# Indexed attention heads: where the softmax reciprocal is applied, in a one-core two-layer trunk

## The chip, the cores and the metric

The kernel runs on one core of a Trainium2 chip. The metric is the device time of one execution in microseconds (us). TensorE (PE) multiplies, VectorE (DVE), ScalarE (ACT) and GpSimd (POOL) do the rest, SyncE (SP) issues most DMAs. Engines run their own instruction streams in order and meet through semaphores. PE writes to eight PSUM banks of 128 partitions by 512 float32.

## The reference

Two decoder layers over 512 tokens of width 1024. Layer 0 mixes 8 forgetting-attention heads (A) with 8 sliding-window heads (B); layer 1 mixes 8 indexed sparse heads (C) with 8 latent heads (D). Each layer then has a squared-ReLU MLP. The part that the change touches is the sparse attention:

```python
logits = jnp.einsum("bqhd,bqkd->bqhk", qb, k_sel) * (d ** -0.5)
logits = jnp.where((dist >= 0)[:, :, None, :], logits + bias, -jnp.inf)
p = jax.nn.softmax(logits, axis=-1)
out = jnp.einsum("bqhk,bqkd->bqhd", p.astype(v_c.dtype), v_sel)
```

Softmax divides each query's exponentials by their sum. The kernel doesn't gather: it scores all causal keys and adds a mask that leaves the selected ones.

## The kernel before, in words

Heads are numbered j = 0 to 31 in the order A, B, D, C, so the indexed heads are j = 24 to 31. Queries lie in four blocks of 128, and a block q attends to its q+1 key blocks, so a head has ten 128x128 blocks of probabilities with queries on the partitions. For `probabilities times values` they must lie with keys on the partitions, so each of the ten is turned on PE into PSUM (`turn_probs`, L993). Precise float32 products are made of rounded halves: a value is split by ACT into a high part and by DVE or POOL into the low rest.

One head passes these stages:

- PE `scores(j)` (L928) into banks 0 to 2; it waits until the exponentials of head j-1 have left each bank.
- DVE `maxima(j)` (L2349): four instructions add the bias strip and find the row maxima, one per query block.
- ACT `exponentials(j)` (L1545) write `probs` and the row sums `expsum`.
- DVE `sums(j)` (L2372) makes the reciprocals `rsum`.
- POOL `diagonal(j)` (L1885), for D and C heads, writes `diag[j % 2]`: four 128x128 diagonal matrices with the reciprocals on them.
- PE `turn_probs(j)`: for A and B heads (whose probabilities DVE has normalised) ten plain transposes (L1021); for D and C heads ten full float32 matmuls of `probs` with `diag` (L1019), which turn and normalise at once. They wait for `diag_made`.
- ACT `probs_hi(j)` (L1535) and DVE `probs_lo(j)` (L2390) copy the three banks of turned probabilities into `probT_h` and `probT_l`.
- PE `values(j)` (L1036) multiplies them with the values (L1031, L1032) into `out_bank(j)`; for C heads rows 0 to 63 hold the product with the high part of the values and rows 64 to 127 that with the low part.
- ACT `output_half(j)` (L1563) copies rows 0 to 63 to SBUF, DVE `outputs_summed(j)` (L2399) adds rows 64 to 127 (L2404) and signals `o_sum`; ACT `output_hi` and POOL `pair_lo` split the result for the output projection.

The heads are software-pipelined. Each engine has its own `heads` function that walks steps s, and the order in a step is written out by hand. In step s of the C stage:

- PE: `scores(s+2)`, `values(s)`, `turn_probs(s+1)`.
- DVE: `probs_lo(s)`, `maxima(s+2)`, `outputs_summed(s-1)`, `sums(s+2)`.
- ACT: `probs_hi(s)`, `output_half(s-1)`, `output_hi(s-2)`, `exponentials(s+2)`, and in steps 24, 26 and 28 the rounding of one weight slab for the output projection.
- POOL: `diagonal(s+1)`, in steps 24, 26 and 28 the low half of that slab, and in odd steps `pair_lo(s-2)`.

`scores` and `maxima` end with head 31, so steps 30 and 31 have none. The output banks of C heads alternate: bank 6 for even j, bank 7 for odd j (`out_bank`, L573). Before `values(j)` overwrites its bank, PE waits for `o_sum` of head j-2 (L1056, `summed_before(j - 1)`); head 25 waits only for the last D head (L1054). `out_projection` (L1167) puts `values(31)` between its first slabs.

Of the kernel before, what the change touches and what calls it, by code (L numbers as in the profile page):

```python
# [28 lines left out]
ALU = mybir.AluOpType  # L29
# [3 lines left out]
P = 128  # L33
D = 1024
# [8 lines left out]
HD = 64  # L43
NH = 8
# [119 lines left out]
def trunk(nc, x, norm_mix_e, w_in_e, b_forget, sink_logits, w_out_e, norm_mix_o, w_in_o, norm_cq, norm_ckv,  # L164
          w_uq, w_ukv, w_out_o, norm_mlp, w_mlp1, w_mlp2, rel_bias, norm_final,
          c_onehot, c_fixed, c_rope, out):
    with ExitStack() as ctx:
        def sb(name, shape, dt=F32):
            return ctx.enter_context(nc.sbuf_tensor(name, shape, dt))

        def sem(name):
            return ctx.enter_context(nc.semaphore(name))

        bank = [ctx.enter_context(nc.psum_tensor(f"bank{i}", [P, 512], F32)) for i in range(8)]
# [5 lines left out]
        ones = sb("ones", [P, P])  # L180
# [110 lines left out]
        diag = [sqsum, sq[:, 1, :]]  # L291
# [63 lines left out]
        exp_done = sem("exp_done")  # L355
        rsum_ready = sem("rsum_ready")
        diag_made = sem("diag_made")
        late_hi = sem("late_hi")
        late_lo = sem("late_lo")
        probs_ready = sem("probs_ready")  # L360
# [6 lines left out]
        o_half = sem("o_half")  # L367
        o_sum = sem("o_sum")
# [94 lines left out]
        def idx_bank(n):  # L463
            return bank[(0, 1, 2, 3, 6, 7)[n % 6]]
# [9 lines left out]
        def unit_of(j, blk):  # L474
            return [u for u in units(j) if u[0] == blk][0]

        def attention(j):
            return "ABDC"[j // NH]

        def score_banks(j):  # L480
            return 2 if attention(j) == "B" else 3

        def banks_before(j):

            return sum(score_banks(i) for i in range(j))

        def pt_parts(j):

            if attention(j) == "B":
                return [(0, 3, 0, 0, 256), (1, 3, 256, 128, 256), (2, 5, 0, 256, 256), (3, 5, 256, 384, 128)]  # L490
            if attention(j) == "A":
                return [(0, 3, 0, 0, 512), (1, 5, 0, 128, 384), (3, 5, 384, 384, 128), (2, 3, 0, 256, 256)]
            return [(0, 3, 0, 0, 512), (1, 4, 0, 128, 384), (3, 4, 384, 384, 128), (2, 5, 0, 256, 256)]
# [9 lines left out]
        def pt_bank_of(j, i):  # L503

            banks = [b for _, b, _, _, _ in pt_parts(j)]
            return sum(1 for k in range(i) if banks[k + 1] != banks[k])

        def pt_before(j):

            return sum(len(pt_banks(i)) for i in range(j))  # L510
# [53 lines left out]
        def summed_before(j):  # L564

            return sum(1 for i in range(j) if attention(i) != "D")
# [6 lines left out]
        def out_bank(j):  # L573

            if j < 2 * NH:
                return bank[6]
            return bank[7] if attention(j) == "D" or j % 2 else bank[6]

        def query_bank(h):

# [225 lines left out]
        def _(pe):  # L806
            mm = nc.tensor.matmul
# [177 lines left out]
            def bank_left(j, k):  # L985

                uses = [(x, y) for x in range(2 * NH * (j // (2 * NH)), j + 1) for y in range(len(pt_banks(x)))
                        if pt_banks(x)[y][0] == pt_banks(j)[k][0] and (x, y) < (j, k)]
                if uses:
                    x, y = uses[-1]  # L990
                    pe.wait_ge(pt_lo, pt_before(x) + y + 1)

            def turn_probs(j, parts_of=lambda kind: range(4)):  # L993
                slot = j % 2
                if j == 0:
                    pe.wait_ge(slab_taken, 3)
                if j == 2 * NH:
                    pe.wait_ge(slab_taken, N_OUT1)
                    pe.wait_ge(dv_lo, 4)

                if j >= 2 * NH:
                    pe.wait_ge(diag_made, j - 2 * NH + 1)
                else:
                    pe.wait_ge(probs_ready, 4 * (j + 1))
                parts = pt_parts(j)
                for i in parts_of(attention(j)):
                    kt, b, col, q0, nq = parts[i]
                    if i == 0 or parts[i - 1][1] != b:
                        bank_left(j, pt_bank_of(j, i))
                    for q in range(q0, q0 + nq, P):  # L1010
                        blk = q // P
                        _, _, _, width, pcol = unit_of(j, blk)
                        if attention(j) == "B":
                            c = pcol + (0 if kt == blk - 1 or blk == 0 else P)
                        else:
                            c = pcol + P * kt
                        dst = bank[b][:, col + q - q0:col + q - q0 + P]
                        if j >= 2 * NH:
                            done = mm(dst, probs[:, slot, c:c + P], diag[slot][:, q:q + P], start=True, stop=True)  # L1019
                        else:  # L1020
                            done = nc.tensor.transpose(dst, probs[:, slot, c:c + P], ident[:, :])  # L1021
                    if i + 1 == len(parts) or parts[i + 1][1] != b:
                        done.then_inc(pt_ready, 1)

            def values_of(j, dst, stationary, check=True):

                for i, (kt, b, col, q0, nq) in enumerate(pt_parts(j)):
                    pe.wait_ge(pt_lo, pt_before(j) + pt_bank_of(j, i) + 1)
                    pc = 512 * pt_bank_of(j, i) + col
                    out_q = dst[:, q0:q0 + nq]  # L1030
                    mm(out_q, stationary(kt), probT_h[:, pc:pc + nq], start=i == 0, stop=False, skip_group_check=not check)  # L1031
                    last = mm(out_q, stationary(kt), probT_l[:, pc:pc + nq], start=False, stop=i == 3,  # L1032
                              skip_group_check=not check)
                last.then_inc(o_ready, 1)

            def values(j):  # L1036

                h = j % NH
                if attention(j) == "D":
                    if j > 2 * NH:  # L1040
                        pe.wait_ge(o_half, j)
                    dst = out_bank(j)[0:HD, :]
                    for i, (kt, b, col, q0, nq) in enumerate(pt_parts(j)):
                        pe.wait_ge(pt_lo, pt_before(j) + pt_bank_of(j, i) + 1)
                        pc = 512 * pt_bank_of(j, i) + col
                        c = P * h
                        last = product(dst[:, q0:q0 + nq], (vd[:, kt, c:c + HD], vd[:, kt, c + HD:c + P]),
                                       (probT_h[:, pc:pc + nq], probT_l[:, pc:pc + nq]), start=i == 0, stop=i == 3)
                    last.then_inc(o_ready, 1)
                else:  # L1050
                    if j == 3 * NH:
                        pe.wait_ge(dk_taken, NH // 2)
                    elif j == 3 * NH + 1:
                        pe.wait_ge(o_half, j - 1)  # L1054
                    else:
                        pe.wait_ge(o_sum, summed_before(j - 1))  # L1056
                    values_of(j, out_bank(j), lambda kt: vc[:, kt, :])

            def first_values(j):

# [127 lines left out]
            for a in range(NQ):  # L1188
                pe.wait_ge(x_loaded[a], 16)
                for half in range(2):  # L1190
                    for k in range(4):
                        last = nc.tensor.transpose(bank[2 * a + half][:, P * k:P * (k + 1)],
                                                   x_tok[a][half][:, P * k:P * (k + 1)], ident[:, :])
# [46 lines left out]
            for a in range(NQ):  # L1240
                last = nc.tensor.transpose(bank[7][:, 8 * a:8 * a + 8], w_scaled[:, P * a:P * (a + 1)],
                                           ident[0:8, 0:8])
            last.then_inc(wi_turned, 1)
            for n, (g, blk) in enumerate(IDX_GROUPS):
# [12 lines left out]
                for a, b in ((0, 0), (0, 1), (1, 0)):  # L1257
                    for i in range(4):
                        rows = slice(32 * i, 32 * (i + 1))
                        last = mm(idx_bank(4 * n + i)[:, 0:w], qi[a][rows, g, qs], ki[b][rows, 0:w], start=(a, b) == (0, 0), stop=a == 1)  # L1260
# [562 lines left out]
        def _(pool):  # L1823
# [60 lines left out]

            def diagonal(j):  # L1885

                if j >= 2 * NH + 2:
                    pool.wait_ge(pt_ready, pt_before(j - 1))
                pool.wait_ge(rsum_ready, j + 1)
                nc.gpsimd.tensor_tensor(diag[j % 2].rearrange("p (a c) -> p a c", a=NQ),  # L1890
                                        ident.unsqueeze(1).to_broadcast([P, NQ, P]),
                                        rsum[:, j % 2, :].unsqueeze(2).to_broadcast([P, NQ, P]),
                                        ALU.mult).then_inc(diag_made, 1)
# [115 lines left out]
        def _(dve):  # L2009
            v = nc.vector  # L2010
            own = Steps(dve, step_v)
# [387 lines left out]
            def outputs_summed(s):  # L2399

                _, r = out_tile(s)
                dve.wait_ge(o_half, s + 1)
                o = o_f32(s)[r:r + HD, :]
                v.tensor_tensor(o, out_bank(s)[HD:P, :], o, ALU.add).then_inc(o_sum, 1)  # L2404

            def last_output_lo():

# [225 lines left out]
```

## Time and profile before

| | us |
|---|---|
| median of 3 runs | 1156.89 |
| lowest and highest | 1156.31, 1157.19 |
| profiled execution, its own time | 1156.44 |
| span of the profiled execution | 1154.6 |
| PE busy in the span | 1116.7 (97%) |
| DVE busy | 880.0 (76%) |
| ACT busy | 614.8 (53%) |
| POOL busy | 387.9 (34%) |

The span runs from the first to the last instruction of the record; 1.8 us of the execution lie around it. A busy PE is an engine with a matmul in its pipeline. Matmuls overlap, so the step from one start to the next is shorter than the duration shown.

### The profile page before, as it was taken

The numbers are of one execution on the slowest core, as the hardware profiler recorded it, in microseconds if no ns is written. First come the engines' busy times: TensorE is split into PE (matmuls) and PEld (weight loads), VectorE is DVE, ScalarE is ACT, GpSimd is POOL, SyncE is SP. The second block draws the span as 40 slices with busy tenths as digits, with TensorE's granted clock in tenths as the row PEclk, the third lists the DMA queues.
The fourth block names the chain that finished last, engine by engine and source line by source line (L and its number), as shares of the span: only waits on it lengthen the run. The fifth ranks groups of instructions, "written<-read, shape, count | busy, mean of one in ns | idle before, by whom it ended". The sixth has DMA issues, their size and how long they took to land.

```text
span 1154.6 us, 16567 instructions
## 1 busy us (share of the span) xinstructions
PE 1116.7 (97%) x6041; PEld 945.2 (82%) x6045; DVE 880.0 (76%) x1484; ACT 614.8 (53%) x1093; POOL 387.9 (34%) x313
## 2 busy tenths in 40 slices
PE   7999998999999999999999999999999999999996
PEld 5788887788989989989967778888878888888885
DVE  5877778678768678668768999656778677787686
ACT  6677677455344354344566377854454453443443
POOL 2444333551131141140175455435521221311400
PEclk9999999999999999999999999999999999999999
DMA  5242441441431521422222100214322424315212
GB/s 165 77 114 81 117 119 47 146 128 55 139 101 53 180 75 49 169 75 70 83 55 74 37 1 25 70 37 158 117 72 79 152 61 146 99 47 182 73 37 91
DMA packets 142226, 105.55 MB, mean 91 GB/s; under 512 B 9078, under 2 KB 122017, under 8 KB 142162
## 3 DMA queue, kind: packets, MB, share of 16 engines
q1 hardware_dynamic: 140892, 104.61, 29.6%
q8 instruction: 34, 0.56, 0.2%
q10 hardware_dynamic: 1270, 0.13, 0.1%
q14 instruction: 30, 0.25, 0.1%
HBM read 102.56 MB, written 6.35 MB: 94 GB/s over the span
## 4 chain that ended last, share of the span: by engine, by line
PE 75%; DVE 15%; ACT 5%; issue 3%; POOL 1%; DMA 1%; SPq 0%; ACTq 0%; DVEq 0%; POOLq 0%
PE bank L811 23%; PE bank L813 23%; PE bank L812 23%; DVE score L2488 2%; DVE best L2484 1%; DVE probT_l L2017 1%; ACT probs L1557 1%; PE bank L1021 1%; ACT ur L1311 1%; PE bank L1019 1%; PE bank L1031 1%; PE bank L1032 1%; POOL wl L1825 1%; DVE bank L2365 1%; DVE xhl L2088 1%
## 5 line engine op out<-in xcount | busy, mean ns | idle before, releaser
L1825 POOL TENSOR_TENSOR wl<-raw,wh 128x512 fp32r<-128x512 f32 x213 | 288.6, 1378 | 596.2 <-ACT wh L1311 560.0
L811 PE MATMUL bank<-ur,wh 128*128 128x512 f32 (+1 forms) x624 | 238.1, 382 | 1.1 <-POOL wl L1825 0.9
L813 PE MATMUL bank<-ur,wl 128*128 128x512 f32 (+1 forms) x624 | 236.3, 379 | 0.0
L812 PE MATMUL bank<-ur,wh 128*128 128x512 f32 x560 | 218.1, 390 | 0.0
L1311 ACT ACTIVATE wh<-raw 128x1024 fp32r<-128x1024 f32 x107 | 111.9, 1053 | 122.4 <-PE bank L813 120.5
L811 PEld LDWEIGHTS bank<-ur,wh 128*128 128x128 f32 x624 | 117.5, 188 | 24.5 <-issue 3.4
L813 PEld LDWEIGHTS bank<-ur,wl 128*128 128x128 f32 x624 | 117.5, 188 | 21.9
L812 PE MATMUL bank<-xhl,wh 128*128 128x512 f32 (+2 forms) x360 | 134.2, 373 | 0.0
L811 PE MATMUL bank<-xhl,wh 128*128 128x512 f32 (+1 forms) x296 | 120.9, 408 | 4.8 <-DVE xhl L2088 3.3
L811 PE MATMUL bank<-ur 128*128 128x256 f32 (+3 forms) x352 | 117.6, 334 | 6.7 <-ACT probs L1557 2.6
L812 PEld LDWEIGHTS bank<-ur,wh 128*128 128x128 f32 x560 | 105.2, 188 | 21.7 <-issue 0.5
L813 PE MATMUL bank<-xhl,wl 128*128 128x512 f32 (+1 forms) x296 | 116.1, 392 | 0.0
L2198 DVE TENSOR_TENSOR xT<-bank,xT 128x512 f32<-128x512 f32 x112 | 74.5, 688 | 51.0 <-PE bank L813 50.9
L1311 ACT ACTIVATE ur<-tbuf 64x512 fp32r<-64x512 f32 (+3 forms) x132 | 75.9, 578 | 67.9 <-DVE tbuf L2225 33.1
L1557 ACT ACTIVATE probs<-bank,negmax 128x256 f32<-128x256 f32 (+3 forms) x128 | 63.2, 505 | 35.1 <-DVE negmax L2368 18.1
L811 PEld LDWEIGHTS bank<-ur 128*128 128x128 f32 x352 | 67.3, 191 | 13.7 <-issue 3.9
L812 PEld LDWEIGHTS bank<-xhl,wh 128*128 128x128 f32 (+1 forms) x360 | 68.0, 189 | 11.8 <-issue 1.0
L813 PE MATMUL bank<-ur 128*128 128x256 f32 (+3 forms) x256 | 77.2, 302 | 0.0
L811 PEld LDWEIGHTS bank<-xhl,wh 128*128 128x128 f32 (+1 forms) x296 | 55.6, 188 | 22.3 <-issue 6.9
L1311 ACT ACTIVATE ur<-probs 128x512 fp32r<-128x512 f32 (+4 forms) x66 | 41.1, 660 | 58.3 <-DVE probs L2232 36.6
L2017 DVE TENSOR_TENSOR probT_l<-bank,probT_h 128x512 fp32r<-128x512 f32 (+1 forms) x88 | 49.5, 600 | 22.3 <-ACT probT_h L1311 22.0
L813 PEld LDWEIGHTS bank<-xhl,wl 128*128 128x128 f32 (+1 forms) x296 | 55.4, 187 | 12.7
(291 smaller groups left out, 2508.1 us busy)
## 6 DMA issues: line engine op xcount, KB each, us to landing
raw<-in_w_mlp SPq DMA_DIRECT2D x64, 512.0 KB, 4.0
raw<-in_w_in_e SPq DMA_DIRECT2D x18, 512.0 KB, 3.7
probs<-in_w_mlp SPq DMA_DIRECT2D x16, 512.0 KB, 4.6
rstd_qk<-in_w_mlp SPq DMA_DIRECT2D x16, 512.0 KB, 4.0
sq<-in_w_mlp SPq DMA_DIRECT2D x16, 512.0 KB, 4.8
raw<-in_w_in_o SPq DMA_DIRECT2D x10, 512.0 KB, 3.7
raw<-in_w_out_e SPq DMA_DIRECT2D x8, 512.0 KB, 3.8
score<-in_w_mlp SPq DMA_DIRECT2D x8, 512.0 KB, 6.1
```

The source lines that it names most:

```text
L811: mm(dst, lhs[0], rhs[0], start=start, stop=False, skip_group_check=not check)
L812: mm(dst, lhs[0], rhs[1], start=False, stop=False, skip_group_check=not check)
L813: return mm(dst, lhs[1], rhs[0], start=False, stop=stop, skip_group_check=not check)
L1019: done = mm(dst, probs[:, slot, c:c + P], diag[slot][:, q:q + P], start=True, stop=True)
L1021: done = nc.tensor.transpose(dst, probs[:, slot, c:c + P], ident[:, :])
L1031: mm(out_q, stationary(kt), probT_h[:, pc:pc + nq], start=i == 0, stop=False, skip_group_check=not check)
L1311: return nc.scalar.activation(dst, src, ACT.Copy, scale=scale)
L1557: e = nc.scalar.activation(probs[:, slot, pc:pc + w], bank[b][:, col:col + w], ACT.Exp, bias=negmax[:, slot, blk:blk + 1], scale=sign, acc ...
L1825: return nc.gpsimd.tensor_tensor(dst, a, b, ALU.subtract)
L2017: return v.tensor_tensor(dst, a, f(b), ALU.subtract)
L2198: v.tensor_tensor(x, t, x, ALU.add).then_inc(product_taken, 1)
L2488: last = v.match_replace(score[:, c0:c0 + w], best8[:, blk - 1, :], score[:, c0:c0 + w], TAKEN)
```

## The change

For C heads PE turns the exponentials by plain transposes, without waiting for the diagonal, and the output is normalised afterwards. A new matmul per head multiplies an all-ones matrix with the head's `diag` (128x512): every row of bank 7 then holds the reciprocals of the 512 queries. `outputs_summed` multiplies the summed output by it. Bank 7 is thus taken, so every C head's output goes to bank 6, and `values(j)` waits for `o_sum` of head j-1. The diagonal's buffer is free again when the ones-matmul of two heads before is done.

```diff
@@ def out_bank(j):
-            return bank[7] if attention(j) == "D" or j % 2 else bank[6]
+            return bank[7 if attention(j) == "D" else 6]
@@ def turn_probs(j):
-                if j >= 2 * NH:
+                if attention(j) == "D":
                     pe.wait_ge(diag_made, j - 2 * NH + 1)
+                elif attention(j) == "C":
+                    pe.wait_ge(exp_done, banks_before(j + 1))
                 else:
                     pe.wait_ge(probs_ready, 4 * (j + 1))
...
-                        if j >= 2 * NH:
+                        if attention(j) == "D":
                             done = mm(dst, probs[:, slot, c:c + P], diag[slot][:, q:q + P], start=True, stop=True)
                         else:
                             done = nc.tensor.transpose(dst, probs[:, slot, c:c + P], ident[:, :])
@@ def values(j):
                     if j == 3 * NH:
                         pe.wait_ge(dk_taken, NH // 2)
-                    elif j == 3 * NH + 1:
-                        pe.wait_ge(o_half, j - 1)
+                        pe.wait_ge(o_half, j)
                     else:
-                        pe.wait_ge(o_sum, summed_before(j - 1))
+                        pe.wait_ge(o_sum, summed_before(j))
                     values_of(j, out_bank(j), lambda kt: vc[:, kt, :])
+                    pe.wait_ge(diag_made, j - 2 * NH + 1)
+                    mm(bank[7][:, :], ones[:, :], diag[j % 2][:, :], start=True, stop=True).then_inc(rows_ready, 1)
@@ def diagonal(j):
-                if j >= 2 * NH + 2:
+                if j >= 3 * NH + 2:
+                    pool.wait_ge(rows_ready, j - 3 * NH - 1)
+                elif j >= 2 * NH + 2:
                     pool.wait_ge(pt_ready, pt_before(j - 1))
@@ def outputs_summed(s):
-                v.tensor_tensor(o, out_bank(s)[HD:P, :], o, ALU.add).then_inc(o_sum, 1)
+                last = v.tensor_tensor(o, out_bank(s)[HD:P, :], o, ALU.add)
+                if attention(s) == "C":
+                    own.link(last)
+                    dve.wait_ge(rows_ready, s - 3 * NH + 1)
+                    last = v.tensor_tensor(o, bank[7][r:r + HD, :], o, ALU.mult)
+                last.then_inc(o_sum, 1)
```

`own.link` lets DVE wait for its own instruction before the next one reads what it wrote.

## Rows read from the trace of the kernel before

**Rows 1.** Busy time by stretch: length, PE, PEld, DVE, ACT, POOL busy; PEclk, DMA share, GB/s.

```profile
727.00:767.00 40.00, 37.97 (x272) 33.07 (x274) 28.27 (x83) 34.58 (x91) 19.71 (x17) 1.00 0.26 73
```

**Rows 2.** Timeline of ACT: start, duration, engine, line, operation, count, idle time before.

```profile
745.39 1.36 ACT L1311 ACTIVATE probT_h<-bank 128x512 fp32r<-128x512 f32 x3
...
750.54 1.59 ACT L1311 ACTIVATE probT_h<-bank 128x512 fp32r<-128x512 f32 x3
...
756.76 1.36 ACT L1311 ACTIVATE probT_h<-bank 128x512 fp32r<-128x512 f32 x3
...
766.01 0.60 ACT L1311 ACTIVATE probT_h<-bank 128x512 fp32r<-128x512 f32 x1 [0.34 <-PE bank L1019]
```

**Rows 3.** Timeline of DVE in the same stage.

```profile
738.10 0.69 DVE L2404 TENSOR_TENSOR rope<-bank,rope 64x512 f32<-64x512 f32 x1
...
743.39 0.70 DVE L2404 TENSOR_TENSOR rope<-bank,rope 64x512 f32<-64x512 f32 x1
...
746.03 1.62 DVE L2017 TENSOR_TENSOR probT_l<-bank,probT_h 128x512 fp32r<-128x512 f32 x3 [1.25 <-ACT probT_h L1311]
747.56 0.29 DVE L2365 CUSTOM_DVE_ANT_0 bank<-bank,strip_raw 128x128 f32<-128x128 f32 x1
...
749.49 0.69 DVE L2404 TENSOR_TENSOR sq<-bank,sq 64x512 f32<-64x512 f32 x1
...
762.55 1.73 DVE L2017 TENSOR_TENSOR probT_l<-bank,probT_h 128x512 fp32r<-128x512 f32 x3 [0.31 <-ACT probT_h L1311]
```

**Rows 4.** Timeline of PE: first matmuls of values, turns, scores and output projection.

```profile
735.48 0.47 PE L1031 MATMUL bank<-probT_h,ur 128*128 128x512 f32 x1
...
741.76 0.58 PE L1031 MATMUL bank<-probT_h,ur 128*128 128x512 f32 x1
...
743.22 2.40 PE L1019 MATMUL bank<-sq,probs 128*128 128x128 f32 x20
745.37 0.30 PE L977 MATMUL bank<-ur,xhl 128*128 128x128 f32 x1
...
747.08 0.58 PE L1031 MATMUL bank<-probT_h,ur 128*128 128x512 f32 x1
...
763.39 0.47 PE L1031 MATMUL bank<-probT_h,ur 128*128 128x512 f32 x1 [0.35 <-DVE probT_l L2017]
...
764.91 2.40 PE L1019 MATMUL bank<-sq,probs 128*128 128x128 f32 x20
767.07 0.47 PE L811 MATMUL bank<-xhl,wh 128*128 128x512 f32 x1
```

**Rows 5.** What PE waited for from 640 to 830 us: total, times, longest.

```profile
PE bank L1019 <- POOL sqsum L1890: 1.7, 3, 0.7
```

**Rows 6.** Timeline of PE at plain transposes of an A head.

```profile
78.56 1.03 PE L1021 MATMUL bank<-fixed,probs 128*128 128x128 f32 x8
79.35 0.31 PE L968 MATMUL bank<-ur 128*128 128x128 f32 x1
```

**Rows 7.** Timeline of PE at an all-ones matmul with a diagonal.

```profile
821.82 1.02 PE L861 MATMUL bank<-sq,ones 128*128 128x512 f32 x2
...
822.91 0.39 PE L812 MATMUL bank<-ur,wh 128*128 128x512 f32 x1
```

**Rows 8.** Timeline of DVE at two instructions joined by `own.link`.

```profile
29.19 0.68 DVE L2141 TENSOR_TENSOR probs<-bank,rstd 64x512 f32<-64x512 f32 x1
29.91 1.35 DVE L2142 TENSOR_SCALAR probs<-probs,bfor 64x512 f32<-64x512 f32 x1
```

**Rows 9.** Timeline of PE around two of its idle stretches.

```profile
10.57 1.09 PE L1192 MATMUL bank<-fixed,score 128*128 128x128 f32 x8
13.83 0.77 PE L811 MATMUL bank<-xhl,wh 128*128 128x512 f32 x1 [2.16 <-DVE xhl L2088]
...
669.91 0.30 PE L811 MATMUL bank<-ur 128*128 128x128 f32 x1 [2.59 <-ACT probs L1557]
```

**Rows 10.** Busy time by stretch, columns as in the first group.

```profile
12.00:15.00 3.00, 1.17 (x3) 1.01 (x4) 2.59 (x6) 2.94 (x5) 0.00 (x0) 0.73 0.63 175
15.00:18.00 3.00, 3.00 (x11) 2.40 (x10) 2.93 (x6) 2.98 (x7) 1.86 (x1) 0.70 0.00 0
655.00:700.00 45.00, 41.27 (x260) 33.54 (x260) 43.14 (x111) 30.17 (x80) 27.38 (x23) 1.00 0.00 1
```

More of the change, by code:

```diff
@@ L357, in trunk @@
         diag_made = sem("diag_made")
+        rows_ready = sem("rows_ready")
         late_hi = sem("late_hi")
```

## The prediction

> **What bounds the kernel now.** I read the busy times by stretch first, then the timelines of ACT, DVE and PE between 727 and 767 us, where the C heads lie, and last the waits of PE. Over those 40 us PE shows 37.97 us busy, ACT 34.58, DVE 28.27 [rows 1]. That looks like a stage bound by PE, but the durations overlap and include time in the pipeline, so the order of starts decides. The reader is to see a ring between ACT and DVE. ACT copies the turned probabilities of head s (745.39 us for head 27), DVE takes their low part 0.64 us later (746.03) and starts the maxima of head s+2 at 747.56; ACT exponentiates head s+2 behind them and then copies head s+1 at 750.54 [rows 2, 3]. The copies start at 745.39, 750.54 and 756.76, so a step lasts 5.15 us, or 6.22 us where ACT also rounds a weight slab; a pair takes 11.37 us, 5.69 us a head [rows 2]. PE works beside the ring. Its only waits for the diagonal are 1.7 us in three places [rows 5].
>
> What matters for the change is the order on DVE within a step: low parts of s, maxima of s+2, and only then the sum of the output of s-1. The output of head 25 is added at 743.39 to 744.09 (step 26), while PE had begun `values(26)` at 741.76; in step 27 the add starts at 749.49, 2.41 us after PE began `values(27)` at 747.08 [rows 3, 4]. Today this is harmless: the two heads write different banks, and `values(s)` waits for the sum of head s-2 only.
>
> **What it removes on PE.** Ten float32 matmuls with the diagonal are 20 instructions; from their first start to the next matmul, 743.22 to 745.37, it is 2.15 us, and 2.16 us for head 31 (764.91 to 767.07) [rows 4]. Eight plain transposes take 79.35 - 78.56 = 0.79 us, so ten take 0.99 us: 1.16 us less a head. The first bank holds four; at a step of (1.03 - 0.27) / 7 = 0.109 us (0.27 us is what is left of the last one: an estimate from the group, 1.03 - 7 x 0.109) they end after 0.60 us [rows 6].
>
> **What it adds on PE.** One all-ones matmul with a diagonal, two instructions. The same operation starts at 821.82, one matmul of 512 columns comes behind it, and the one after that starts at 822.91. The usual step of such a matmul is about 0.23 us, so the pair takes 822.91 - 821.82 - 0.23 = 0.86 us [rows 7]. PE's own work thus falls by 1.16 - 0.86 = 0.30 us a head, 2.4 us over eight heads. No more than that, and the 1.7 us of waits for POOL, can be had from PE; the ring hides nearly all of it.
>
> **What it adds on DVE.** One 64x512 multiplication of PSUM with SBUF behind a link. The link: an instruction of 0.68 us at 29.19 lets the next start at 29.91, so 0.04 us [rows 8]. The multiplication has the shape of the add: 0.69 us [rows 3]. Together 0.73 us behind the add. The rows of bank 7 were made right after the values of that head, long before, so their wait ends early. By itself the multiplication would fall into the idle time before the low parts (1.25 or 0.31 us [rows 3]) and cost little, at most 0.73 us a head.
>
> **The new wait.** `values(s)` now writes the same bank 6 as `values(s-1)` and waits for `o_sum` of head s-1. Behind it on PE's queue stand the ones-matmul, `turn_probs(s+1)` and `scores(s+3)`; ACT's copies of s+1, and then DVE's, wait for those turns. And the sum of s-1 stands on DVE behind the low parts of s and all maxima of s+2. So DVE no longer works beside PE: the two alternate. POOL's `diagonal(s+1)` now waits for the ones-matmul of s-1, with a slab's low half and `pair_lo` queued behind it; PE has done that matmul a step earlier, so this costs nothing here. The loop from one `values` to the next, at the full clock:
>
> - values(s): 743.22 - 741.76 = 1.46 us [rows 4]
> - ones-matmul: 0.86 us [rows 7]; its diagonal, for which PE waits at most 0.7 us today [rows 5], now has a step more, so it isn't late
> - first four transposes: 0.60 us [rows 6]
> - PE to ACT: 8 of 20 turns of head 31 end at about 764.91 + 1.06 = 765.97, ACT starts at 766.01: 0.04 us [rows 2, 4]
> - ACT's first copy until DVE starts: 746.03 - 745.39 = 0.64 us [rows 2, 3]
> - low parts: 747.56 - 746.03 = 1.53 us [rows 3]
> - four maxima: 749.49 - 747.56 = 1.93 us [rows 3]; the scores for them follow the turns on PE and are ready in time
> - add with link, multiplication: 0.73 + 0.69 = 1.42 us [rows 3, 8]
> - DVE to PE: the first low part ends at 762.55 + 0.69 = 763.24, `values(30)` starts at 763.39: 0.15 us [rows 3, 4]
>
> Sum 8.63 us, against 5.69 now. ACT's exponentials and weight slabs lie beside it with over 2 us to spare, so the two step lengths become one.
>
> Where it starts and ends: the first wait that binds is at head 25, which PE began at 735.48. The add of head 24 starts at 738.10, so `values(25)` starts at 738.10 + 1.42 + 0.15 = 739.67 [rows 3, 4]. Four loops of 8.63 us lead to `values(29)` at 774.19. Step 30 has no maxima: 8.63 - 1.93 = 6.70 us, so `values(30)` at 780.89. It was at 763.39 [rows 4]: 17.5 us later. From there PE is the bound in both: the turns of head 31 save 1.17 us, and the ones-matmuls of heads 30 and 31 add 1.72 us. The 0.73 us more of DVE behind `values(31)` lie beside seven tiles of output projection. In all 17.5 - 1.17 + 1.72 = 18.1 us (rounded). The profiled execution took 1156.44 us: 1174.5 us at a full clock.
>
> **The clock.** PE now stands still in each loop for 8.63 - (1.46 + 0.86 + 0.99 + 1.71) = 3.6 us; the last term is a head's scores, 745.37 to 747.08 [rows 4]. The gap before head 25 is about 5 us, that before head 30 about 3.4. The trace shows two idle stretches nearly as long. At 669.91 PE had been idle for 2.59 us and the granted clock stayed at 1.00. At 13.83 it had been idle for 2.16 us, and the clock fell to 1.2 GHz: means of 0.73 and 0.70 over two stretches of 3 us make (0.27 + 0.30) x 2 x 3 = 3.4 us at that level [rows 9, 10]. The new gaps are longer than both and come six times, so I expect the clock to fall in most. A fall covers 3.4 us by that row; half of it, 1.7 us, is lost where PE is on the path, which it is for 2.9 us after each gap. The price of one gap lies between 0 and 1.7 us for one fall (2.9 if the clock doesn't come back in time). In the row the fall began 3.4 us before it ended, some 0.4 us ahead of the first matmul, which leaves 3.0 / 2 = 1.5 us; I take 1.4, as part of a fall may lie on the ACT and DVE leg. Six gaps cost 8.4 us: 1174.5 + 8.4 = 1182.9 us, and as the median of the runs is 0.45 us above the profiled one, 1183.
>
> The Trainium skill ("TensorE: Matmul & The Clock Gate", section "HAM oscillation — how this bites in real kernels") says that bursts of matmuls with a wait between them can each begin at the low clock, every time anew. By that rule the six gaps pay; without it the sum is 1174.5. Its section "Part 4: PE-mode transpose" adds that transposes don't count as work for the clock. Here eight transposes ran at 10.57 with a step of 0.109 us, full speed after nothing but transposes, so this trace speaks against it; if it holds, the price goes towards the last rival below.
>
> **The rivals.**
>
> *The clock holds.* For it: the 2.59 us without a fall. Against: the 2.16 us with one. Then 1174.9 us over the median.
>
> *The clock stays low through the stage.* PE's leg of 1.46 + 0.86 + 0.60 = 2.92 us doubles in all six loops: 17.5 us instead of 8.4, 1192 us. Against it: the one fall of the trace ended with the first dense work.
>
> *The wait finds its sum ready.* The other side: bank 6 is free when PE asks. Then the ring stays at 5.69 us, and PE's 2.4 us and waits for POOL are what can be gained: at best 1156.9 - 2.4 = 1154.5, or no change if the ring hides it. It would decide if `o_sum(s-1)` were ready before 747.08 in step 27, that is if DVE added before the maxima. The rows have the add at 749.49 and the multiplication behind it, 3.8 us too late. Only a mistake of mine about the order speaks for it.
>
> *Part of the delay is given back*, since weights for the output projection are loaded and split earlier against PE. PE waits there hardly at all now, so a microsecond at most; it is within the range.
>
> **How the numbers follow.** Clock falls in most gaps 0.67 (own range 1178 to 1187), clock holds 0.19, clock low throughout 0.11, wait not binding 0.03 (half faster, half same). Two tenths of a per cent, 2.3 us, is what a measurement can tell here. The range from 1172 to 1190 takes in the case at full clock with 3 us for errors in the loop. Slower 0.97, faster 0.01, same 0.02.
>
> **What would show it.** In the changed profile: PE waiting before L1031 for DVE's multiplication, about 3 us in each of six places; `values` starting every 8.6 to 10 us between heads 25 and 29; turns at 0.99 us and the ones-matmul at 0.86 us at full clock; no wait of PE for POOL's diagonal; the granted clock below 1.00 from 735 to 790. The prediction is wrong if the multiplications are done before PE comes to `values`, if the step of the ring is still under 6.5 us, or if the clock is 1.00 throughout and the time is still far from 1175.

## The result and the profile after

| | us |
|---|---|
| median after (4 runs, 1183.43 to 1186.27) | 1185.37 |
| median before (4 runs) | 1157.04 |
| ratio, with its 95% interval | 1.0241 [1.0228, 1.0254] |
| profiled execution after, and its span | 1185.21, 1183.4 |

The change makes the kernel 28.3 us slower; 1183 was forecast. The place is the stage of the indexed heads. First the busy times from 735 to 795 us, with the columns of [rows 1], before and after: the granted clock, the figure after POOL's, falls from 1.00 to 0.80. "Low clock" below is TensorE's lower level, 1.2 GHz instead of 2.4.

```profile
735.00:795.00 60.00, 57.97 (x338) 49.22 (x339) 37.79 (x85) 38.58 (x90) 28.12 (x23) 1.00 0.20 58
```

```profile
735.00:795.00 60.00, 40.12 (x175) 28.91 (x176) 28.03 (x76) 29.78 (x77) 18.73 (x16) 0.80 0.15 44
```

Next what PE waited for between 725 and 800 us (total, times, longest). The three waits for POOL of [rows 5] are gone; in their place come six waits for L2414, the new multiplication.

```profile
PE bank L1034 <- DVE rope L2414: 13.5, 4, 4.3
PE bank L1034 <- DVE sq L2414: 6.4, 2, 3.3
```

The timeline of PE at the first matmul of `values(25)` to `values(30)`, the counterpart of [rows 4]. The bracket gives the idle time before and its releaser; every one of the six names the multiplication. A "gap" below is such an idle time, a "loop" the time from one of these starts to the next.

```profile
741.75 0.79 PE L1034 MATMUL bank<-probT_h,ur 128*128 128x512 f32 x1 [4.33 <-DVE rope L2414]
...
752.46 0.50 PE L1034 MATMUL bank<-probT_h,ur 128*128 128x512 f32 x1 [3.37 <-DVE rope L2414]
...
762.55 0.50 PE L1034 MATMUL bank<-probT_h,ur 128*128 128x512 f32 x1 [3.13 <-DVE sq L2414]
...
772.56 0.50 PE L1034 MATMUL bank<-probT_h,ur 128*128 128x512 f32 x1 [3.27 <-DVE sq L2414]
...
782.51 0.50 PE L1034 MATMUL bank<-probT_h,ur 128*128 128x512 f32 x1 [2.97 <-DVE rope L2414]
...
790.49 0.50 PE L1034 MATMUL bank<-probT_h,ur 128*128 128x512 f32 x1 [2.81 <-DVE rope L2414]
```

One loop on PE, between two of these, and then DVE in the same loop. At 744.26 the ones-matmul shows 1.91 us where [rows 7] has 1.02 for the same form: the low clock. The turns that follow it wait for nothing, but they are late. DVE has stood idle for 5.75 us when its low parts begin at 747.53, does its maxima, and only at 750.99 the add and at 751.72 the multiplication. 0.74 us after that one's start PE goes on.

```profile
744.26 1.91 PE L1061 MATMUL bank<-sq,ones 128*128 128x512 f32 x2
745.96 1.55 PE L1024 MATMUL bank<-fixed,probs 128*128 128x128 f32 x10
747.27 0.31 PE L978 MATMUL bank<-ur,xhl 128*128 128x128 f32 x1
```

```profile
747.53 1.62 DVE L2023 TENSOR_TENSOR probT_l<-bank,probT_h 128x512 fp32r<-128x512 f32 x3 [5.75 <-ACT probT_h L1315]
749.06 0.29 DVE L2371 CUSTOM_DVE_ANT_0 bank<-bank,strip_raw 128x128 f32<-128x128 f32 x1
...
750.99 0.69 DVE L2410 TENSOR_TENSOR rope<-bank,rope 64x512 f32<-64x512 f32 x1
751.72 0.69 DVE L2414 TENSOR_TENSOR rope<-bank,rope 64x512 f32<-64x512 f32 x1
```

Where the 28.8 us of the span went, by the starts of the same instructions in both traces. The stage begins later already: DVE's low parts of head 24 start at 730.71 after and at 728.54 before.

```profile
728.54 1.62 DVE L2017 TENSOR_TENSOR probT_l<-bank,probT_h 128x512 fp32r<-128x512 f32 x3 [0.81 <-ACT probT_h L1311]
```

```profile
730.71 1.62 DVE L2023 TENSOR_TENSOR probT_l<-bank,probT_h 128x512 fp32r<-128x512 f32 x3 [0.81 <-ACT probT_h L1315]
```

| stretch | before | after | difference |
|---|---|---|---|
| up to the low parts of head 24 | 728.54 | 730.71 | +2.17 |
| from there to `values(25)` | 6.94 | 11.04 | +4.10 |
| `values(25)` to `values(30)` | 27.91 | 48.74 | +20.83 |
| `values(30)` to the output projection (767.07, 795.37) | 3.68 | 4.88 | +1.20 |
| the rest | | | +0.5 |

The first line lies ahead of all changed code and is put down to no part of the change. It has two parts. In this execution the clock fell at another point of the start (mean 0.76 between 17 and 24 us), and the idle stretch of [rows 9] ends at 671.08 instead of 669.91, 1.17 us later. Behind that same gap of 2.59 us the clock then fell too, which it had not done before (mean 0.96 between 655 and 700 us, against 1.00 in [rows 10]); that is the other 1.00 us.

```profile
17.00:24.00 7.00, 5.57 (x16) 3.99 (x17) 4.02 (x13) 2.43 (x4) 0.00 (x0) 0.76 0.28 75
```

```profile
655.00:700.00 45.00, 41.48 (x255) 33.79 (x254) 42.20 (x110) 29.43 (x75) 25.65 (x21) 0.96 0.00 1
```

Such differences go with the spread between runs of one kernel: of the runs of the kernel before that were taken beside the experiments, those with a mean clock of 0.997 took 1156.0 to 1157.2 us, the two with 0.993 took 1158.7 and 1159.3.

### The profile page after: what moved, and what is told of

Its sections match the earlier page's. It is cut to its first block, busy times and chain, and to the rows that moved or that the text cites. A ratio compares the mean times of both kernels' runs of the same rounds, so it can differ in the third digit from the quotient of the medians.

```text
span 1183.4 us, 16455 instructions
## 1 busy us (share of the span) xinstructions
PE 1126.2 (95%) x5977; PEld 945.6 (80%) x5981; DVE 884.5 (75%) x1492; ACT 615.4 (52%) x1093; POOL 388.0 (33%) x313
## 4 chain that ended last, share of the span: by engine, by line
PE 78%; DVE 13%; ACT 4%; issue 3%; DMA 1%; POOL 1%; SPq 0%; DVEq 0%; ACTq 0%
PE bank L812 23%; PE bank L814 23%; PE bank L813 23%; PE bank L1024 2%; PE bank L1034 1%; PE bank L1035 1%; PE bank L1022 1%; DVE score L2499 1%; DVE bank L2371 1%; DVE best L2495 1%; DVE probT_l L2023 1%; PE bank L1061 1%; ACT ur L1315 1%; ACT probs L1561 1%; DVE xhl L2094 1%
## 5 line engine op out<-in xcount | busy, mean ns | idle before, releaser
L1561 ACT ACTIVATE probs<-bank,negmax 128x256 f32<-128x256 f32 (+3 forms) x128 | 63.2, 505 | 35.1 <-DVE negmax L2374 18.1
```

Of the source, the lines that this page charges most:

```text
L1561: e = nc.scalar.activation(probs[:, slot, pc:pc + w], bank[b][:, col:col + w], ACT.Exp, bias=negmax[:, slot, blk:blk + 1], scale=sign, acc ...
```

## The experiments

The theory: the single output bank makes `values(s)` wait for a sum that stands behind the maxima on DVE's queue, so PE and DVE alternate, and each gap of PE lets the clock fall besides. The rivals: the added instructions cost the time; the clock plays no part; PE bounded the stage all along. Ratios are to the kernel before, run on the same chip.

**e1, the wait alone**, on the kernel before:

```diff
-            return bank[7] if attention(j) == "D" or j % 2 else bank[6]
+            return bank[7 if attention(j) == "D" else 6]
...
-                    elif j == 3 * NH + 1:
-                        pe.wait_ge(o_half, j - 1)
                     else:
-                        pe.wait_ge(o_sum, summed_before(j - 1))
+                        pe.wait_ge(o_sum, summed_before(j))
```

> The kernel before with one part of the change: all indexed heads write bank 6 and values(s) waits for the sum of head s-1. Turns with the diagonal, no ones-matmul, no multiplication. Theory (the wait makes PE and DVE alternate): the loop is 1.46 + 1.06 (eight of twenty turns) + 0.04 + 0.64 + 1.53 + 1.93 + 0.69 + 0.15 = 7.5 us, values(25) at 738.94, values(30) 11.1 us later than before, about 1168 us at a full clock; PE's idle gap is then only 2.2 us, so falls of the clock may add up to 7 us (1175). Rival (the ones-matmul and the multiplication themselves cost the time): about 1157.

1173.86 us (1171.50 to 1177.52), ratio 1.0143 [1.0122, 1.0164]. With none of the added instructions, 16 of the 28 us are there. PE's `values` in its trace:

```profile
740.07 0.80 PE L1031 MATMUL bank<-probT_h,ur 128*128 128x512 f32 x1 [3.25 <-DVE rope L2402]
...
750.49 0.50 PE L1031 MATMUL bank<-probT_h,ur 128*128 128x512 f32 x1 [2.11 <-DVE rope L2402]
...
758.10 0.50 PE L1031 MATMUL bank<-probT_h,ur 128*128 128x512 f32 x1 [2.02 <-DVE sq L2402]
...
765.71 0.50 PE L1031 MATMUL bank<-probT_h,ur 128*128 128x512 f32 x1 [2.26 <-DVE sq L2402]
...
774.93 0.50 PE L1031 MATMUL bank<-probT_h,ur 128*128 128x512 f32 x1 [2.02 <-DVE rope L2402]
```

Two loops in a row take 7.61 us (7.5 was worked out). The loop that begins at 740.07 takes 10.42, and its first matmul shows 0.80 us instead of 0.50: it ran at the low clock (low from 739.5 to 746.4). The loop behind the gap of 2.26 us takes 9.22, those behind 2.11 and 2.02 us take 7.61: such gaps let the clock fall in some loops and not in others, which fits the spread of 6 us between the runs (argued, only one of the runs has a trace).

**e2, the plain turns alone**, on the changed kernel (ones-matmul, multiplication and the single bank with its waits taken out again, of which the cut shows the multiplication). The indexed heads' output is left without its division by the softmax sum, so this kernel only serves to measure time:

```diff
-                last = v.tensor_tensor(o, out_bank(s)[HD:P, :], o, ALU.add)
-                if attention(s) == "C":
-                    own.link(last)
-                    dve.wait_ge(rows_ready, s - 3 * NH + 1)
-                    last = v.tensor_tensor(o, bank[7][r:r + HD, :], o, ALU.mult)
-                last.then_inc(o_sum, 1)
+                last = v.tensor_tensor(o, out_bank(s)[HD:P, :], o, ALU.add)
+                last.then_inc(o_sum, 1)
```

> The other part alone: indexed heads are turned by plain transposes that wait for the exponentials, banks 6 and 7 alternate with the old waits, and the ones-matmul and the multiplication are left out, so the indexed heads' output is not normalised. Theory: the ring between ACT and DVE stays at 5.69 us a head, PE's 1.16 us a head are hidden except for the last turns: 1155 to 1157. Rival (PE's work bounds the stage, and the saved 8 x 1.16 us count): 1148 to 1150.

1157.61 us (1155.77 to 1160.89), ratio 1.0000 [0.9991, 1.0009]. PE's saving is hidden. ACT's copies of the turned probabilities, as in [rows 2], start every 5.16 or 6.10 us (before: 5.15 and 6.22). Only the long steps got 0.12 us shorter. That also rules out POOL as the bound of the long steps: it makes a slab's low half and then the diagonal there, but in e2 no turn waits for the diagonal.

```profile
740.72 1.37 ACT L1314 ACTIVATE probT_h<-bank 128x512 fp32r<-128x512 f32 x3
...
746.82 1.37 ACT L1314 ACTIVATE probT_h<-bank 128x512 fp32r<-128x512 f32 x3
...
751.98 1.37 ACT L1314 ACTIVATE probT_h<-bank 128x512 fp32r<-128x512 f32 x3
```

**e3, the sum before the maxima**, one edit on the changed kernel:

```diff
+                    if s > 3 * NH:
+                        outputs_summed(s - 1)
                     if first <= s + 2 < last:
                         maxima(s + 2)
-                    if s > 3 * NH:
-                        outputs_summed(s - 1)
```

> The changed kernel with one edit: in a step DVE takes the sum of head s-1 before the maxima of head s+2. Theory (the place of the sum on DVE's queue decides): the loop over PE is 8.63 - 1.93 = 6.70 us, in the two steps with a weight slab the ring of ACT and DVE is longer, 6.22 + 1.42 = 7.64 us; values(30) about 10 us later than in the kernel before, 1167 us, up to 1170 with a few falls of the clock. Rival (the extra work is what costs): no change from the changed kernel, 1185.

1171.24 us (1169.73 to 1174.12), ratio 1.0124 [1.0108, 1.0139]. An order of two calls on DVE gives back 14 us, half of the loss, with every added instruction still there. After a first loop at the low clock (9.33 us) the loops take 7.74, 6.65, 7.74 and 6.64 us, against 7.64 and 6.70 worked out:

```profile
747.58 0.50 PE L1034 MATMUL bank<-probT_h,ur 128*128 128x512 f32 x1 [1.29 <-DVE rope L2414]
...
755.32 0.50 PE L1034 MATMUL bank<-probT_h,ur 128*128 128x512 f32 x1 [2.45 <-DVE sq L2414]
...
761.97 0.50 PE L1034 MATMUL bank<-probT_h,ur 128*128 128x512 f32 x1 [1.55 <-DVE sq L2414]
```

**e4 and e5, the clock held up.** PE fills its gaps with matmuls that nobody reads ("fillers"), on the changed kernel:

```diff
                     else:
+                        pe.wait_ge(pt_lo, pt_before(j + 1))
+                        for _ in range(13):
+                            mm(bank[5][:, 256:384], ones[:, :], ident, start=True, stop=True)
                         pe.wait_ge(o_sum, summed_before(j))
```

> The changed kernel with PE kept busy: after the low parts of head s are taken, 13 float32 matmuls of ones with the identity go to unused columns of bank 5 before the wait for the sum, 13 x 0.213 = 2.8 us of a gap of 3.4. They write nothing that is read. Theory (each gap costs 1.4 us by a fall of the clock): the granted clock stays at 1.00 in the stage and the loops are 8.6 to 8.7 us, 1176 to 1178 us. Rival (the gaps cost nothing by the clock, the loop's terms were too short): 1185 or more.

1179.45 us (1178.76 to 1179.49), ratio 1.0185 [1.0169, 1.0200]: above the 1176 to 1178 us expected, because head 31 has no gap, and its fillers lay on the path (from `values(30)` to `values(31)` it takes 10.93 us in e4 and 8.13 in e5). e5 leaves them out there (`range(13 if j < 4 * NH - 1 else 0)`).

> e4 without its 13 filler matmuls at head 31, where there was no gap to fill and they lay on PE's path. Theory (falls of the clock cost the difference between the changed kernel and a loop at full clock): 1179.4 - 2.8 = 1176.6 us, clock 1.00 in the stage, some 9 us under the changed kernel. Rival (the fillers cost time in the gaps too): 1179.

1175.58 us (1174.75 to 1175.67), ratio 1.0155 [1.0140, 1.0171]. PE does 78 matmuls more than in the changed kernel, and the kernel is 9.8 us faster. It could be faster still: step 30 has no maxima, so the multiplication starts there at 779.24, but the fillers run on and `values(30)` starts at 781.46, 1.5 us later than a handover of 0.74 us would give. The stretch and one loop of e5's trace: clock 1.00, no idle time worth a bracket before `values`, 756.46 - 748.02 = 8.44 us a loop against 9.95 to 10.71 in the changed kernel.

```profile
735.00:795.00 60.00, 56.38 (x364) 47.06 (x367) 31.70 (x82) 31.01 (x79) 19.05 (x17) 1.00 0.14 40
```

```profile
748.02 0.50 PE L1034 MATMUL bank<-probT_h,ur 128*128 128x512 f32 x1
...
749.41 1.02 PE L1064 MATMUL bank<-sqsum,ones 128*128 128x512 f32 x2
750.27 1.26 PE L1024 MATMUL bank<-fixed,probs 128*128 128x128 f32 x10
751.28 0.31 PE L978 MATMUL bank<-ur,xhl 128*128 128x128 f32 x1
...
753.21 3.17 PE L1060 MATMUL bank<-fixed,ones 128*128 128x128 f32 x26
756.46 0.50 PE L1034 MATMUL bank<-probT_h,ur 128*128 128x512 f32 x1
```

**e6, the bank given back after the add:**

```diff
-                        pe.wait_ge(o_sum, summed_before(j))
+                        pe.wait_ge(o_added, j - 3 * NH)
...
                     pe.wait_ge(diag_made, j - 2 * NH + 1)
+                    if j > 3 * NH:
+                        pe.wait_ge(o_sum, summed_before(j))
...
-                    own.link(last)
+                    last.then_inc(o_added, 1)
+                    dve.wait_ge(o_added, s - 3 * NH + 1)
```

> The changed kernel with one edit: bank 6 is given back after the add and not after the multiplication (a semaphore of its own); the ones-matmul waits for the multiplication of the head before. Theory: 0.73 us less in each loop, so the seven waits shrink by 0.7 us each, 5 us less where the clock falls as often: 1180 us, and less if shorter gaps (2.9 us) let it fall less often, down to 1173. Rival (the multiplication lies beside other work already): 1185.

1176.29 us (1173.95 to 1178.51), ratio 1.0161 [1.0143, 1.0179]: 9 us off the changed kernel, between the 5 us of the shorter loop alone and the 12 of a clock that holds. Both happened: the loop is shorter, and the clock holds in some loops. The first `values` start at 741.56, 750.75, 760.12, 767.83, 777.18 and 783.09. The loop of 7.71 us is 8.44 - 0.73; those of 9.19, 9.37 and 9.35 are it plus 1.5 to 1.7.

```profile
760.12 0.50 PE L1035 MATMUL bank<-probT_h,ur 128*128 128x512 f32 x1 [2.40 <-DVE sq L2413]
...
767.83 0.50 PE L1035 MATMUL bank<-probT_h,ur 128*128 128x512 f32 x1 [2.63 <-DVE sq L2413]
...
777.18 0.50 PE L1035 MATMUL bank<-probT_h,ur 128*128 128x512 f32 x1 [2.40 <-DVE rope L2413]
```

**e7, normalised afterwards without losing a bank.** On the changed kernel, `out_bank` and its waits as before. The values leave out the product of the two low halves and fill only rows 0 to 63, the reciprocals go to rows 64 to 127 of the same bank, and on DVE the multiplication takes the place of the add:

```diff
-                    values_of(j, out_bank(j), lambda kt: vc[:, kt, :])
+                    dst = out_bank(j)[0:HD, :]
+                    for i, (kt, b, col, q0, nq) in enumerate(pt_parts(j)):
+                        pe.wait_ge(pt_lo, pt_before(j) + pt_bank_of(j, i) + 1)
+                        pc = 512 * pt_bank_of(j, i) + col
+                        last = product(dst[:, q0:q0 + nq], (vc[:, kt, 0:HD], vc[:, kt, HD:P]), ...
...
-                    mm(bank[7][:, :], ones[:, :], diag[j % 2][:, :], start=True, stop=True).then_inc(rows_ready, 1)
+                    mm(out_bank(j)[HD:P, :], ones[:, 0:HD], diag[j % 2][:, :], start=True, stop=True).then_inc(rows_ready, 1)
```

> The same new normalisation without the shared bank: the values are multiplied as for the latent heads (three products into partitions 0 to 63, low times low left out), the reciprocals' rows go to partitions 64 to 127 of the same bank, one multiplication takes the place of the add, and banks 6 and 7 alternate with the old waits. Theory (the bank and its wait are the cause, not the normalisation afterwards): PE needs 1.71 + 1.94 + 0.86 + 0.99 = 5.5 us a head, the ring 5.15 or 6.1: 1157 to 1159. Rival (the ones-matmul and the later multiplication are the cost): over 1165.

1158.74 us (1158.26 to 1161.30), ratio 1.0018 [1.0009, 1.0027]. Plain turns, ones-matmul and a late multiplication cost 1 to 2 us (1.35 by the medians, 0.18% by the ratio) and not 28 when two banks alternate. It isn't the added work one for one: the second DVE instruction, 0.73 us a head, is missing, and `values` are longer on PE. The loops are 5.80 us, and PE waits for nothing between them: now PE is the bound.

```profile
741.09 0.58 PE L812 MATMUL bank<-probT_h,ur 128*64 128x512 f32 x1
...
746.89 0.58 PE L812 MATMUL bank<-probT_h,ur 128*64 128x512 f32 x1
```

**e8, the weight slabs out of the ring**, on the kernel before:

```diff
-SPARE_STEP1 = 28
-OUT_SPLIT_STEPS = {24: 0, 26: 1}
+SPARE_STEP1 = 30
+OUT_SPLIT_STEPS = {20: 0, 21: 1}
```

> The kernel before with the three weight slabs of the output projection rounded in steps 20, 21 and 30 instead of 24, 26 and 28. It tests that a ring of ACT and DVE sets the stage before the change. Theory: the long steps of 6.22 us lose their 1.06 us of ACT; PE's own 5.32 us a head are then the bound: values(30) about 2.3 us earlier, 1154 to 1155.5. Rival (PE bounds the stage already): 1157.

1156.00 us (1155.23 to 1157.83), ratio 0.9986 [0.9977, 0.9995]: the one version that beats both kernels, by 0.14%. The long steps are gone, and `values` start every 5.31 to 5.33 us, PE's own 5.32.

```profile
744.60 0.58 PE L1031 MATMUL bank<-probT_h,ur 128*128 128x512 f32 x1
...
749.91 0.58 PE L1031 MATMUL bank<-probT_h,ur 128*128 128x512 f32 x1
...
755.24 0.58 PE L1031 MATMUL bank<-probT_h,ur 128*128 128x512 f32 x1
```

From `values(25)` to `values(30)` it takes 25.44 us instead of 27.91; Part of these 2.5 us is lost ahead of the stage, where two of the slabs are handled now. Measured against the changed kernel's trace, which has the same early falls of the clock, e8 is 0.2 us late at 671.28; from there to `values(24)` it loses 1.6 us more (733.96 against 732.14), and one turn of a D head waits for POOL, which it does in neither of the other traces there:

```profile
716.58 2.50 PE L1019 MATMUL bank<-sqsum,probs 128*128 128x128 f32 x20 [0.87 <-POOL sqsum L1890]
```

**e9, e3 and e6 together:**

> The changed kernel with the edits of e3 and e6 together: DVE sums and multiplies before the maxima, and bank 6 is free after the add. Theory: the loop over PE falls to 8.44 - 1.93 - 0.73 = 5.8 us, under the ring of ACT and DVE, which the early sum lengthens by 1.42 us to 6.57 us (7.6 with a weight slab); the loops become those 6.6 and 7.6 us, as in e3, PE's gaps are shorter, 1167 to 1171 us: hardly better than e3. Rival (the two repairs add up as they do alone, 14 and 9 us): 1162.

1168.57 us (1165.35 to 1169.93), ratio 1.0101 [1.0084, 1.0118]. The two repairs don't add up (that would be 1162): the loops are 6.60, 7.76, 6.61, 7.75 and 6.61 us, those of e3, and all at full clock in the profiled execution, which is the fastest of the four. They fit the ring of ACT and DVE with 1.42 us more in it (5.15 + 1.42 = 6.57). The clock stays at 1.00 even behind the longest gap, in front of `values(30)`:

```profile
772.33 0.50 PE L1035 MATMUL bank<-probT_h,ur 128*128 128x512 f32 x1 [3.12 <-DVE rope L2413]
```

## Why the prediction was right

*What bounded the stage.* A ring of ACT and DVE, with PE close beside it. e2 (PE's turns shortened, nothing gained) and e8 (three roundings taken off ACT, PE's 5.32 us appear) show both halves.

*The wait.* Right in place and cause, and 0.19 us a loop too dear. `values(25)` comes 4.10 us later than the stage's own start would put it (4.19 predicted). The loop at full clock is 8.44 us in e5 (8.63 predicted). Its terms there: values 1.39, ones-matmul 0.86, four turns to ACT 0.64, ACT to DVE 0.62, low parts and maxima 3.46, add with link 0.73, multiplication and handover 0.74. Two terms were mis-sized. For the values 1.46 us were taken from a loop in which PE doesn't wait; here it is 1.39. And 0.15 us were given to the way from DVE to PE, from the start of `values(30)`; it is about 0.05. The remaining 0.02 us lie between ACT and DVE.

*The added work.* 0.86 us for the ones-matmul and 1.01 for ten turns (751.28 - 750.27) are as predicted, at full clock. In e7, where nothing waits for the bank, normalising afterwards costs 1 to 2 us, with one DVE instruction less than in the change.

*The clock.* The direction was right, and the size, 1.4 us a gap, some 0.2 us too small. Against the 8.44 us of e5 the four full loops of the changed kernel take 10.71, 10.09, 10.01 and 9.95, so 2.3 to 1.5 us more. The 2.3 belong to the first gap, behind which the clock was low for twice as long (739.7 to 746.6) as behind the others. The prediction took it that part of a fall would lie ahead of the first matmul or on the leg of ACT and DVE, where it costs nothing. But behind the other five gaps the fall begins 0.4 to 1.6 us into PE's work (after the start at 752.46 it is low from 753.3 to 756.9), so nearly all of it is paid.

The Trainium skill ("TensorE: Matmul & The Clock Gate", section "HAM oscillation — how this bites in real kernels") was cited for the rule that each burst starts at the low clock again. The trace agrees that the clock falls once more for each of the six gaps, but not that the burst starts low: of the six first matmuls only that at 741.75 shows 0.79 us, the others 0.50 as at full clock. And the gaps of e9 let it fall not once.

*The sum.* 18.1 for loop and edges and 8.4 for the clock were forecast, 26.5 in all. Measured from the low parts of head 24 on it is 28.8 - 2.2 = 26.6 us. That the two agree to 0.1 us is luck, for two errors cancel. e5 tells them apart. `values(24)` starts there at 729.98 (before: 729.94), its span is 1173.0 - 1154.6 = 18.4 us longer, and 1.5 of that are its own fillers in step 30. So the delay at full clock is 16.9 us and not 18.1, and the clock costs 26.6 - 16.9 = 9.7 us and not 8.4. The 2.2 us ahead of the stage were not foreseen.

*The rivals.* That the wait finds its sum ready is refuted by the six brackets. A full clock with gaps was wrong for this kernel, though in e1, e3 and e6 it held for part of the loops and in e9's trace for all. A clock low throughout was wrong too: the scores of each loop show full-speed durations. (This is the rival that the prediction means where it speaks of transposes that don't count as work; it stands second in its list, not last.) Nothing was given back behind the stage: the rest of the kernel takes 0.5 us more.

## What to carry to other kernels

Before a change takes a buffer away, look up where on its consumer's queue the instruction stands that gives it back: here the add stood behind two microseconds of unrelated work, harmless with two banks; with one, moving it ahead of that work gives back 14 of the 28 us. Work saved on an engine that a ring between two others hides is worth nothing until the ring is shorter. And where a new wait leaves TensorE idle for a few microseconds in each loop, the loss of clock can come on top: here about 10 of the 28 us by e5.

## What the runs showed of the hardware

- In the changed kernel gaps of 2.8 to 4.3 us made the clock fall each time. Of the ten gaps between 2.0 and 2.7 us in e1 and e6 three did (2.26, 2.63, 2.64). In e3 one of 2.51 us did, and those of 2.44, 2.45 and even 3.14 didn't; in e9 the clock stayed at 1.00 through gaps of up to 3.12 us. A gap of 2 to 3 us costs 0 or about 1.6 us, and its length alone doesn't tell which.
- The idle stretch of 2.59 us in [rows 9] shows this without any change to its code: it has the same length in all eleven traces (here at 671.08, 670.09, 670.47, 670.68, 670.28 and 671.28 in the changed kernel, e1, e2, e4, e6 and e8), and in these six the clock falls around it, in the kernel before, e3, e5, e7 and e9 it doesn't. What decides was not found.
- Matmuls whose result nobody reads made a kernel 9.8 us faster (e5), with the granted clock at 1.00 instead of 0.80 over 60 us.
- A plain float32 transpose of 128x128 is one instruction with a step of 0.10 us (ten in 1.01 us, e5); the same turn as a product with a diagonal is two instructions and 0.215 us (ten in 2.15 us, [rows 4]).
